# Where the last modulation table's pieces stand on VectorE in the second layer's feed-forward part

## The reference, cut to what matters

```python
mod = jax.nn.silu(c) @ w_ada + b_ada
sh1, sc1, gt1, sh2, sc2, gt2 = [m[:, None, :] for m in jnp.split(mod, N_MOD, axis=-1)]
...
h = _rmsnorm(x, g_pre_ffn) * (1.0 + sc2) + sh2
f = (jax.nn.silu(h @ w_gate) * (h @ w_up)) @ w_down
return x + gt2 * _rmsnorm(f, g_post_ffn)
```

## Time and profile before

| | |
|---|---|
| median of 3 runs | 842.99 us (842.76 to 843.09) |
| the profiled execution, its own time | 842.83 us |
| its span, first to last instruction | 841.0 us |
| TensorE busy | 831.0 us, 99% of the span |
| VectorE busy | 687.9 us, 82% |
| ScalarE busy | 459.0 us, 55% |
| GpSimd busy | 119.3 us, 14% |
| granted TensorE clock | 0.998 |
| loads of pieces (80 in all), issue to landing, median | 5.8 us |

### The profile page before, as it was taken

How to read it: one execution, slowest core, us unless ns; L and a number is a source line. 1 busy time by engine, 2 the same in 40 slices (tenths; PEclk the granted TensorE clock), 3 DMA queues, 4 the chain that set the end, 5 groups by cost and what they waited for, 6 DMA issues and landing times.

```text
span 841.0 us, 11584 instructions
## 1 busy us (share of the span) xinstructions
PE 831.0 (99%) x4131; PEld 689.2 (82%) x4131; DVE 687.9 (82%) x1180; ACT 459.0 (55%) x732; POOL 119.3 (14%) x92
## 2 busy tenths in 40 slices
PE   8999999999999999999999999999999999999997
PEld 6877888888888888888888788888888788788885
DVE  5898889888787777787689899988787887989984
ACT  5675555565657433434476555465565745454542
POOL 5500300301210012030320040040040000000002
PEclk9999999999999999999999999999999999999999
DMA  8996666576317788777437756766643396165362
GB/s 347 404 368 237 212 262 249 202 268 233 130 73 297 277 285 314 277 290 301 173 126 283 290 207 222 264 219 242 240 146 118 146 347 233 51 258 192 150 226 75
DMA packets 34795, 194.09 MB, mean 231 GB/s; under 512 B 4273, under 2 KB 4529, under 8 KB 17714
## 3 DMA queue, kind: packets, MB, share of 16 engines
q1 hardware_dynamic: 33410, 189.64, 61.0%
q0 software_dynamic: 1328, 3.71, 1.3%
HBM read 192.29 MB, written 1.05 MB: 230 GB/s over the span
## 4 chain that ended last, share of the span: by engine, by line
PE 92%; DMA 3%; DVE 2%; issue 1%; ACT 1%; SPq 0%; DVEq 0%
PE ps L1735 24%; PE ps L1737 23%; PE ps L1736 23%; PE ps L2154 5%; PE ps L1848 4%; DMA wide_t<-scale_first 3%; PE ps L1912 2%; PE ps L1772 1%; PE ps L1773 1%; PE ps L1779 1%; PE ps L1933 1%; PE ps L1934 1%; PE ps L1894 1%; PE ps L1911 1%; PE ps L1932 1%
## 5 line engine op out<-in xcount | busy, mean ns | idle before, releaser
L1156 DVE TENSOR_TENSOR w_lo<-raw,w_hi 128x2048 fp32r<-128x2048 f32 (+2 forms) x126 | 288.2, 2294 | 55.4 <-ACT w_hi L769 54.1
L1735 PE MATMUL ps<-w_hi,t_hi 128*128 128x512 f32 (+2 forms) x712 | 282.0, 396 | 1.6 <-DVE w_lo L1156 1.0
L1737 PE MATMUL ps<-w_hi,t_lo 128*128 128x512 f32 (+2 forms) x712 | 275.1, 386 | 0.0
L1736 PE MATMUL ps<-w_lo,t_hi 128*128 128x512 f32 (+2 forms) x712 | 274.5, 386 | 0.0
L769 ACT ACTIVATE w_hi<-raw 128x2048 fp32r<-128x2048 f32 (+2 forms) x128 | 240.5, 1883 | 33.0 <-DMA raw<-w_stream 26.9
L666 POOL PARTITION_ALL_REDUCE wide_t<-wide_t x20 | 77.0, 3849 | 591.7 <-DVE wide_t L1281 590.8
L1735 PEld LDWEIGHTS ps<-w_hi,t_hi 128*128 128x128 f32 x712 | 133.8, 188 | 30.4 <-DVE w_lo L1156 2.9
L1737 PEld LDWEIGHTS ps<-w_hi,t_lo 128*128 128x128 f32 x712 | 133.7, 188 | 27.6
L1736 PEld LDWEIGHTS ps<-w_lo,t_hi 128*128 128x128 f32 x712 | 134.0, 188 | 25.1
L1281 DVE SCALAR_TENSOR_TENSOR wide_t<-ada,cs,wide_t 128x1024 f32<-128x1024 f32 x80 | 110.2, 1378 | 0.4
L1735 PE MATMUL ps<-w_hi,m_hi 128*128 128x512 f32 x208 | 84.6, 407 | 0.3 <-DVE m_lo L1455 0.3
(11 more groups left out here) (257 smaller groups left out, 1072.9 us busy)
## 6 DMA issues: line engine op xcount, KB each, us to landing
raw<-w_stream SPq DMA_DIRECT2D x124, 1024.0 KB, 5.4
ada<-w_ada SPq DMA_DIRECT2D x80, 512.0 KB, 5.8
wide_t<-gains POOLq DMA_DIRECT2D x7, 512.0 KB, 4.6
mixed<-w_stream SPq DMA_DIRECT2D x3, 1024.0 KB, 8.5
raw<-w_stream SPq DMA_DIRECT2D x4, 656.0 KB, 6.8
mixed<-scale_first SPq DMA_DIRECT2D x2, 1024.0 KB, 10.3
wide_t<-shift_first SPq DMA_DIRECT2D x4, 512.0 KB, 10.9
wide_t<-scale_first SPq DMA_DIRECT2D x2, 1024.0 KB, 12.5
```

The source lines that it names most:

```text
L1156: nc.vector.tensor_tensor(w_lo[:, U % RING, a:n], src[:, a:n], w_hi[:, U % RING, a:n].bitcast(F32), ALU.subtract).then_inc(s_lo, 1)
L1735: nc.tensor.matmul(dst, hi, w_h, start=first, stop=False)
L1736: nc.tensor.matmul(dst, hi, w_l, start=False, stop=False)
L1737: return nc.tensor.matmul(dst, lo, w_h, start=False, stop=last)
```

## The change

One of the pieces (number 76) goes from block 3 to the pair 5, 6. In a pair all pieces stand behind the last low part (`m_lo_split` of the second block). For the pair 8, 9 this moves piece 77 behind one `split_lo` and two `m_lo_split`; pieces 78 and 79 stand where they stood. SyncE's order follows the list: the load of piece 76 leaves the place in block 3 and comes in the pair 5, 6 between the last unit but one and the last, which is the first unit of the next pair (into `mixed`). Loads 77 to 79 keep their places. GpSimd's program is the same.

```diff
@@ ffn_pieces(l)
     if l + 1 < DEPTH:
         return (0, 2, 3, 3, 3, 3, 3, 3, 2, 2, 0), (4, 8)
-    return (1, 1, 2, 1, 0, 0, 0, 0, 3, 0, 0), (10,)
+    return (1, 1, 2, 0, 0, 1, 0, 0, 3, 0, 0), (10,)
@@ twin_lo(l, j)
                 split_lo(l, behind[6])
-                add_pieces(min(many, 1))
                 split_lo(l, behind[7])
                 m_lo_split(l, j + 1, 0)
                 m_lo_split(l, j + 1, 1)
-                add_pieces(max(many - 1, 0))
+                add_pieces(many)
```

## The result

The changed kernel takes 844.43 us (median of 20 runs, 843.45 to 845.96) against 843.04 us (20 runs, 842.47 to 843.18) for the kernel before. The ratio is 1.0018, 95% interval 1.0012 to 1.0024. That is 1.4 us more, a small loss. It is just inside the 0.2% that I counted as no change, but clear of noise, and nearly twice the 0.74 us that I had worked out. The runs of the changed kernel also spread over 2.5 us, those of before over 0.7.

What follows compares the result with a forecast made beforehand. TensorE, busy 99% of the 841.0 us span, was taken as the bound. The terms -0.79 (block 4), 0 (pair 5, 6) and +1.53 (finish) gave +0.74 on 842.99: 843.7 us, range 842.7 to 845.0.

Steps and rivals of the forecast that it cites:

- Block 4: Without piece 76 in block 3, VectorE's chain runs earlier and TensorE's stall at block 4's turns shrinks: -0.79 us.
- Pair 5, 6 on VectorE: Piece 76's 1.19 us fit into VectorE's 1.32 us of idle time behind the last `m_lo_split`: 0.
- Pair 5, 6, the load: Piece 76's load delays `mixed` by 1.26 us, the low part by 0.29; block 7's margin of 0.34 holds: 0.
- the first rival: Block 4's relief doesn't arrive, or an equal stall arises in block 7: +1.53 us, 844.5 us, chance 0.15.
- Pair 8, 9: Piece 79's load waits for piece 77, so piece 79 ends 2.71 us later; `gate_m` of block 10 behind it is hidden.
- The finish: The last table comes 2.71 us later, tile 1's finish follows tile 0's without a wait, and the end is +1.53 us.
- The sum: All terms over the whole kernel: -0.79 + 0 + 1.53 = +0.74 us, 843.7 us for the median.
- The reduction: GpSimd's sums behind piece 79 stay at 6.56 us; with the mean of 8.62 and 6.56 the end is 1.03 us later.

Runs made afterwards that it cites:

- load_in_block_3: Against the kernel before, only piece 76's VectorE instruction moves to the pair 5, 6; its load stays in block 3: 842.03 us, ratio 0.9990.
- the second set: The changed kernel measured once more, unaltered, on another chip beside the kernel before: 844.11 us, ratio 1.0014.
- extra_load: The kernel before plus an unused 512 KB load on SyncE's queue in the pair 5, 6, ahead of the load into `mixed`: 843.33 us, ratio 1.0008.

## Why the prediction was right or wrong

**Block 4: right.** The step said -0.79 us, limited by ScalarE's high part and not by the piece's 1.19 us. VectorE's chain shows 0.78 in the trace, the stall is gone, and with the load out of the way the whole kernel is 0.86 us faster.

**Pair 5, 6 on VectorE: right.** The piece fits in the idle time and costs nothing (load_in_block_3).

**Pair 5, 6, the load: this is the step that failed.** The prediction named it as a sign that it was wrong: "if a turn in block 7 waits". I priced the load of piece 76 at 1.26 us, made the low part 0.29 us late, left a margin of 0.34 us in block 7, and took 0. The transfer's price was about right in the mean (1.2 us). Three things were missing. SyncE needs 0.48 us to issue the load, and `mixed` waits in the same queue: a term that I should have counted, since a step that is moved takes its issue along. The landing times scatter by some 0.7 us, which is more than the margin was. The margin itself would have been 0.28, had I taken off the 0.06 us from a product's end to its turn, as I did for block 4. In the profiled execution `mixed` was 2.2 us late in place of 1.26, and TensorE waited 0.62 us. That is the first rival, which had 0.15: "a new one of the same size arises in block 7". It gave 844.5 us; 844.43 were measured, in the second set 844.11. The match to 0.07 us is in part luck: the wait comes in some executions only (three of the five traces that have the load here and block 4 relieved), and a little of the loss is the finish's.

**Pair 8, 9: right.** VectorE waits 2.1 us for the load of piece 79 (2.3 expected), and the load lands 3.4 us after its issue. Piece 79 ends at 821.55 in place of 818.72, 2.83 us later; measured against TensorE's last matmul, which came 0.19 us earlier, that is 3.02 where 2.71 was the forecast. What is queued behind it, `gate_m` of block 10, is hidden.

**The finish: right in its mechanism, a little short.** Measured the same way, the end is 1.56 + 0.19 = 1.75 us later, where 1.53 were forecast. The load of the last unit adds 0.3 us (4.9 us against 4.6) and that of the gains 0.1 (4.1 against 3.9); tile 1's finish gives 0.2 back, as it takes 3.10 us behind tile 0's and not 3.32. I had treated the loads' times as fixed, and in a chain without slack each late one counts in full. It should also move the median, though no run isolates that: the 4.6 us of the trace before are the shortest of twelve, whose median is 5.0.

**The sum.** -0.19 + 1.75 = +1.56 us in the profiled execution, where I had -0.79 + 1.53. The medians, 1.39 and 1.11 us over the kernel before, lie between the forecast and the first rival. The range, 842.7 to 845.0, holds both.

**The reduction** took 6.55 to 6.57 us in every trace of this study, with the few VectorE instructions of block 10 beside it, not the 8.62 of the earlier table. The Trainium skill's rule on the shared ports ("SBUF — State Buffer", the section on two separate sides) agrees with that: those instructions read one operand from PSUM. Beside the earlier table's sums a piece, with its operands in SBUF, took 3.27 us (at 564.39) in place of 1.28. For the gains' load, which GpSimd issues, the Trainium skill ("DMA: Bandwidth & Descriptors", anatomy of one DMA) gives 2.0 us and the bytes over 436 GB/s, an estimate of 3.2 us for 512 KB; the traces here have 3.9 to 4.1, so the measured one is to be used.

## What to carry to other kernels

When an instruction is moved, its load moves too, and the load's price is its issue plus its transfer plus their scatter, paid by whatever is queued behind it. Here it was best to leave the load where it was and to move only the compute: -0.86 us, where moving both gave -0.57.

With two buffers, putting three pieces in one place exposes the third one's load: its issue waits for the first of the three. Spread them, or give the last one a place of its own.

A margin of a few tenths of a microsecond ahead of a load that scatters by more is no margin. Price it as partly paid.

## What the runs showed that I had not expected

One and the same load of 1 MB, the last unit's, took 4.6 to 6.8 us to land in the twelve traces of these nearly equal programs. The order of before hides most of that. In extra_load, which has that order and the 6.8 us, the table is made 1.58 us later than in the earlier trace rows and the last addition ends 0.19 us later. The kernel before spreads over 0.7 us in its 20 runs and over 1.0 and 1.6 in the sets on the third and the first chip; the changed one hands a late load on to the end, and its runs spread over 2.5 and 2.3 us.
